# Final normalisation of a decoder step: two of five output tiles multiplied on ScalarE and GpSimd, and the outputs stored in another order

## What is computed

```python
h = h + moe_ffn(rms_norm(h, ffn_norm_g), ...)
y = rms_norm(h, final_norm_g)

def rms_norm(x, g):
    y = x * lax.rsqrt(jnp.mean(x * x, axis=-1, keepdims=True) + RMS_EPS)
    return y * g
```

## Time and profile before

| | us |
|---|---|
| three runs | 1114.21, 1114.60, 1118.05 |
| median | 1114.6 |
| the profiled execution's own time | 1114.37 |
| its span, first to last record | 1112.8 |
| end of the last expert's matmuls | 1078.9 |
| first and last gather of the tail issued | 1082.3, 1095.6 |
| first tile's square begins | 1097.05 |
| last multiply of VectorE ends | 1109.4 |

### The profile page before, as it was taken

The page is one execution under the profiler, slowest core; times in us unless marked ns, Lnnn a source line. Parts: engine busy times, 40 slices in busy tenths (PEclk is TensorE's granted clock), DMA queues, the critical chain, the costliest instruction groups (busy, mean ns, idle before and its releaser), DMA issues.

```text
span 1112.8 us, 11560 instructions
## 1 busy us (share of the span) xinstructions
PE 943.7 (85%) x4412; PEld 509.4 (46%) x4412; DVE 338.7 (30%) x743; ACT 201.7 (18%) x445; POOL 198.8 (18%) x296
## 2 busy tenths in 40 slices
PE   7978999989999998899976998788778888787860
PEld 6634444767776566674543433333333333232320
DVE  2269999973341111330144100000000000000006
ACT  3243111213343233000121000000000000000012
POOL 2730650100001200000231122111111111111113
PEclk9989999999999999999996999999998998999995
DMA  9920221611204527923035999999999999999947
GB/s 333 392 80 0 76 81 41 232 34 43 76 1 151 196 108 204 374 80 151 38 123 212 410 416 423 423 425 426 425 422 424 424 428 423 424 423 425 403 179 249
DMA packets 52102, 283.72 MB, mean 255 GB/s; under 512 B 8508, under 2 KB 9376, under 8 KB 32855
## 3 DMA queue, kind: packets, MB, share of 16 engines
q1 hardware_dynamic: 41223, 246.21, 55.2%
q0 software_dynamic: 10784, 36.97, 9.1%
q10 hardware_dynamic: 56, 0.01, 0.0%
HBM read 267.38 MB, written 23.17 MB: 261 GB/s over the span
## 4 chain that ended last, share of the span: by engine, by line
PE 62%; DVE 18%; DMA 7%; issue 7%; ACT 4%; SPq 1%; POOL 0%; ACTq 0%; POOLq 0%; DVEq 0%; PEldq 0%
PE psum L1021 20%; PE psum L1036 10%; PE psum L783 9%; DVE arena L1424 6%; DVE arena L1422 6%; PE psum L937 5%; PE psum L919 4%; DMA arena<-in_w_exp_up 3%; DMA arena<-in_w_branch_pool 3%; PE psum L607 3%; PE psum L871 1%; PE psum L1029 1%; DVE arena L1650 1%; PE psum L837 1%; ACT arena L1094 1%
## 5 line engine op out<-in xcount | busy, mean ns | idle before, releaser
L1021 PE MATMUL psum<-arena 128*64 128x512 f32 x992 | 238.4, 635 | 54.5 <-issue 51.7
L1021 PEld LDWEIGHTS psum<-arena 128*64 128x64 f32 x992 | 85.5, 146 | 205.7 <-issue 204.1
L1036 PE MATMUL psum<-arena 128*64 128x512 f32 x512 | 116.9, 597 | 17.7 <-ACT arena L1320 17.7
L783 PE MATMUL psum<-arena 128*128 128x288 f32 x480 | 126.0, 415 | 0.0
L783 PEld LDWEIGHTS psum<-arena 128*128 128x128 f32 x480 | 89.6, 192 | 30.9 <-issue 8.1
L1650 DVE TENSOR_TENSOR arena<-arena,psum 128x256 f32<-128x256 f32 x32 | 13.5, 421 | 289.4 <-ACT arena L1316 289.4
L593 PE MATMUL psum<-arena 128*128 128x512 f32 x192 | 86.2, 604 | 2.1 <-ACT arena L1187 2.1
L1316 ACT ACTIVATE arena<-psum 128x256 f32<-128x256 f32 x32 | 12.3, 384 | 415.5 <-PE psum L1021 404.8
L1036 PEld LDWEIGHTS psum<-arena 128*64 128x64 f32 x512 | 40.4, 136 | 72.1 <-issue 70.7
L1654 DVE COPY arena<-psum 128x512 f32<-128x512 f32 x32 | 22.1, 692 | 157.1 <-PE psum L1036 157.1
L919 PE MATMUL psum<-arena 128*128 128x288 f32 x256 | 64.3, 415 | 5.1 <-DMA arena<-in_w_branch_pool 5.1
(11 more groups left out here) (263 smaller groups left out, 930.9 us busy)
## 6 DMA issues: line engine op xcount, KB each, us to landing
arena<-in_w_exp_down SPq DMA_DIRECT2D x32, 2048.0 KB, 22.9
arena<-in_w_exp_gate SPq DMA_DIRECT2D x30, 2048.0 KB, 18.7
arena<-in_w_exp_up SPq DMA_DIRECT2D x29, 2048.0 KB, 22.8
arena<-in_w_in SPq DMA_DIRECT2D x7, 2048.0 KB, 8.8
y_d<-arena SPq DMA_DIRECT2D x1, 8192.0 KB
arena<-in_w_exp_up SPq DMA_DIRECT2D x6, 1024.0 KB, 15.1
arena<-in_x_prompt SPq DMA_DIRECT2D x8, 512.0 KB, 7.5
arena<-in_w_out SPq DMA_DIRECT2D x2, 2048.0 KB, 7.7
```

The lines of the kernel that those rows point to most:

```text
L783: last = pe.matmul(bank(2 + n % 2 if n < SAMPLE_G else 2, HN), ring[slot % 2][:, k, m * P:(m + 1) * P], xnT[:, k, HN * hh:HN * hh + HN], s ...
L1021: last = pe.matmul(bank(2 + s, 512, rows).rearrange("p (w n) -> p w n", w=2), x_k, wgu[s][:, :, DE * k + 256 * q:DE * k + 256 * q + 256], ...
L1036: last = pe.matmul(bank(4 + s, 512, slice(64 * half, 64 * half + 64)), hT[s][:, k % 2, CAP * (k // 2):CAP * (k // 2) + CAP], wd[s][:, k, 5 ...
```

## The change

Tiles 0 and 1 lose the multiply on VectorE (L1679). ScalarE now scales them by their row numbers (as L1304 does), in its list behind the square root of tile 1 and of tile 2; GpSimd multiplies them in place by `fgrow` behind its last gather. Their reciprocals stay on VectorE. `sp` stores the tiles in the order 2, 0, 3, 1, 4; `fin_ready` now counts tiles 2, 3 and 4 only, and `xn2_r` and `xs2_r` go on from 5.

```diff
-            for i in range(TILES):
-                sp.wait_ge(S["fin_ready"], i + 1)
+            for i in (2, 0, 3, 1, 4):
+                if i < 2:
+                    sp.wait_ge(S["xn2_r"], TILES + i + 1)
+                else:
+                    sp.wait_ge(S["fin_ready"], i - 1)
                 sp.dma_start(y_rows[i], yout[i][0:rows_of(i), :]).then_inc(S["y_out"], 16)
...
                 act.activation(rt3[0:r, i:i + 1], ss3[0:r, i:i + 1], ACT.Sqrt, bias=eps[0:r], scale=1.0 / D).then_inc(S["rt3"], 1)
+                if 1 <= i <= 2:
+                    act.wait_ge(S["rs3"], i)
+                    act.activation(yout[i - 1], resid[:, i - 1, :], ACT.Copy, scale=rstd3[:, i - 1:i]).then_inc(S["xs2_r"], 1)
...
-                dve.scalar_tensor_tensor(yout[i][0:r, :], resid[0:r, i, :], rstd3[0:r, i:i + 1], fgrow[0:r, :], ALU.mult, ALU.mult).then_inc(S["fin_ready"], 1)
+                if i >= 2:
+                    dve.scalar_tensor_tensor(yout[i][0:r, :], resid[0:r, i, :], rstd3[0:r, i:i + 1], fgrow[0:r, :], ALU.mult, ALU.mult).then_inc(S["fin_ready"], 1)
...
                 combine(1, y_d[0:FIRST, :])
+            for i in range(2):
+                pool.wait_ge(S["xs2_r"], TILES + i + 1)
+                pool.tensor_tensor(yout[i], yout[i], fgrow, ALU.mult).then_inc(S["xn2_r"], 1)
```

## The result

The changed kernel takes 1118.62 us in the median of 20 runs (1116.15 to 1120.78), the kernel before 1114.76 in the median of 20 (1111.66 to 1118.05). The ratio is 1.0030, 95% interval 1.0022 to 1.0038: **slower by 3.3 us, between 2.5 and 4.2**. That is small, but clear of no change. The profiled execution took 1118.96, its span 1117.4.

What follows compares the result with a forecast made beforehand. The experts wait for weights; the change touches only the last 16 us, paced by VectorE's chain to tile 4's add. +2.2 for that add and +0.4 for stores, on 1114.37, gave 1117.0 us, range 1113.3 to 1118.8.

Steps and rivals of the forecast that it cites:

- rival B: Final stores queue fully, tile 4 behind tile 1 (1.1), and GpSimd's multiplies are the long ones: +3.7, 1118.0; chance 0.12.
- ScalarE's queue: In the tail, copies delay squares and roots, so VectorE waits for root 2; without GpSimd's effect, tile 4's add moves -1.3.
- The copies give 1.1 back: ScalarE's two copies in the tail cut the gain at tile 4's add from 2.4 to 1.3 us.
- about 0.7: Sign in the changed profile: VectorE idle this many us before reciprocal 2, waiting for root 2.
- The full stop: In the tail each GpSimd multiply halts VectorE, which ends 1.1 us after it; tile 4's add moves +2.2.
- near 2.4 and near 3.4: Signs: VectorE's multiply 2 lasts near 2.4 us instead of 1.28, tile 4's add (or multiply 3) near 3.4.
- The stores: At the end, tile 1's store ahead of tile 4's delays tile 4's landing: 0.4 us taken, between 0 and 1.1.
- 0.35 us later the span ends: At the program's end, the span closes this long after tile 4's store lands, 1112.45 in the kernel before.
- the sum of the text: Tail total: +2.2 for the last add and +0.4 for the stores, +2.6, giving time 1117.0.
- Rival A: GpSimd and VectorE don't stop each other at 1024 columns; tile 4's add moves -1.3, time 1113.3; chance 0.18.

Runs made afterwards that it cites:

- e1: The changed kernel without GpSimd's two multiplies, tiles 0 and 1 stored without the gain; 1114.60 us, ratio 0.9999 to the kernel before.
- e7: e1 without ScalarE's two copies too, tiles 0 and 1 stored unnormalised; a single execution, not timed, span end 14.12 us after square 0.
- e2: The changed kernel with the gain row copied to PSUM, where VectorE's three multiplies read it; 1118.17 us, ratio 1.0029 to the kernel before.
- e3: e2 with the first adds of tiles 3 and 4 also writing their sums to PSUM; 1115.77 us, ratio 1.0014 to the kernel before.

## Why the prediction was right, and where it fell short

The forecast was 1117.0, slower by 2.6; measured were 1118.6 and 3.3 by the ratio. Direction and range held; the forecast's own ends, 1116.2 to 1117.7, did not. The range held partly by luck: 1118.62 lies 0.2 below its upper bound of 1118.8, which was put past rival B's value, and what lengthened the program was not rival B. The times alone don't tell 2.6 from 4.0, as their interval is 2.5 to 4.2; the rows of the tail do.

- *ScalarE's queue.* Right: VectorE waited for root 2, and without GpSimd the add would have come 1.42 earlier than before (e1), where 1.3 was forecast. A copy takes 1.13 (1.15 taken). "The copies give 1.1 back" put down too much to them: e1 against e7 gives 0.74, and 0.24 is root 2's own time behind tile 2's add, which no copy causes. The wait before reciprocal 2 was 0.34 in the changed kernel, "about 0.7" was forecast, because the gather of tile 3 landed later and took the other part of the same wait; in e1 it was 0.65.
- *The full stop, priced at 1024 columns from rows of 256 and 384.* Right in kind and size: VectorE ended 1.10 and 1.08 after GpSimd, 1.1 was forecast; GpSimd's rows 3.2 and 3.3, VectorE's 2.76 and 3.35, "near 2.4 and near 3.4" were forecast. e2 and e3 show that it is VectorE's two SBUF inputs that meet GpSimd: the same operation with one input in PSUM kept 1.28 beside it. The section "Who interferes with whom" of the page "SBUF — State Buffer" of the Trainium skill says the same: with two SBUF inputs a VectorE instruction contends with a GpSimd instruction that reads SBUF, with at most one it doesn't. Tile 4's add moved by 2.15 (11.51 against 9.36); 2.2 was forecast.
- *The stores.* Right: 3.5 to landing against 3.0, 0.4 was taken. Rival B's 1.1 did not occur.
- *The end.* Here the prediction failed: "0.35 us later the span ends" took the landing for the only end of the program. With it the changed span would have ended at 1115.7 + 0.35 = 1116.05, 18.39 after square 0, which is +2.64: the sum of the text. It ended at 19.74, since GpSimd's closing row, 9.1 us from its last instruction, had passed the landing: 19.74 - 18.39 = 1.35 of the 4.0 us come from a term that the sum doesn't have. **GpSimd's work was costed by what it stops and not by when it ends.** The row was in the profile of the kernel before, with 7 us to spare. That GpSimd "has nothing to do after that" should have been read as 7 us of cover that the change would use up: it moved GpSimd's last instruction by 11.0 (from -0.56 to 10.43).
- *Rival A.* What it assumed, no stop, was made in e3, and its 1113.3 would not have come then either: 1115.8, because of the drain. Of the changed kernel's 4.0 us, 1.7 go when the stop goes (GpSimd ends at 10.43 against 8.71), and 2.3 stay in e3, where only the drain is left to cause them. That is more than the 1.35 above, because without the stop the last landing would come earlier too.

## What to carry to other kernels

In the last 10 us of this program GpSimd is not free even where it stands idle: its last instruction plus about 9.3 us was a floor under the end in all of its forms. So look up each engine's closing row, not only the last landing, before work is moved there. GpSimd's tensor_tensor on SBUF took turns with VectorE's scalar_tensor_tensor of two SBUF inputs (2.76 and 3.35 us in place of 1.28); with one of VectorE's inputs in PSUM each kept its own time. Moving work from a full engine to two others is worth what the next wait leaves: here 2.4 us off VectorE would have come to 1.4 at its last add, and to 0.9 at the end of the span, even with GpSimd for nothing (e1).

## What was not expected of the hardware

The DRAIN row that closes a program on GpSimd ends 9.0 to 9.1 us after the end of its last instruction in all eleven kernels, be that a gather, a multiply of 2.35 us or a memset of 0.10 us after 13 us of idleness; on ScalarE it is 0.32, on SyncE 0.013. The profile puts SyncE's wait behind it down to TensorE's queue ("SPq L150 <- PEq L150"), whose own closing row had begun at 1076.5 and lasted 2.3. What GpSimd does in the 9 us, the runs don't show, nor how long the closing row is in another kernel. Every run on record has its span recorded too, so none shows the row without recording.
